# Moving the split weight rings by 32 bytes in a matmul-bound decoder layer

## The reference, cut to what matters

```
x = LN(a*x + 0.5*FFN1(x))        FFN: (silu(x @ w_gate) * (x @ w_up)) @ w_down, width 5632
x = LN(a*x + Mixer(x))
x = LN(a*x + 0.5*FFN2(x))
Mixer: z = x @ w_in -> q, k, v | c_b, c_c, c_h | g_attn, g_conv
       y_attn = differential attention (8 heads; prompt causal, sample over paged caches) @ w_attn_out
       y_conv = (c_b * short_conv(c_c * c_h)) @ w_conv_out
       (sigmoid(g_attn) * y_attn + sigmoid(g_conv) * y_conv) @ w_o
```

## Time and profile before

| | |
|---|---|
| median of 3 runs | 2275.51 us (2274.4 to 2275.91) |
| the profiled execution's own time | 2274.37 us |
| its span, first to last instruction | 2272.6 us |
| TensorE matmul busy | 2258.4 us, 18574 matmuls |
| VectorE busy | 1366.7 us |
| ScalarE busy | 998.0 us |
| DMA | 475 MB, mean 209 GB/s |

### The profile page before, as it was taken

One profiled execution on the slowest core, in us unless ns is written; L12 is line 12 of the kernel. 1 busy time (PEld: TensorE's weight loads), 2 busy tenths in 40 slices (PEclk: granted clock), 3 DMA queues, 4 the chain that ended last, 5 costly groups with the idle time before them and its releaser, 6 DMA issues.

```text
span 2272.6 us, 45670 instructions
## 1 busy us (share of the span) xinstructions
PE 2258.4 (99%) x18574; PEld 2227.3 (98%) x18574; DVE 1366.7 (60%) x1523; ACT 998.0 (44%) x1236; POOL 29.8 (1%) x59
## 2 busy tenths in 40 slices
PE   9999999999999999999999999999999999999997
PEld 9999999999999999999998899999999999999997
DVE  5444454444655689999975457886444444445554
ACT  5344444443434454455543454554444444434333
POOL 1000000000000001000000000000000000000001
PEclk9999999999999999999999999999999999999999
DMA  7655555555555688989988855555555555555553
GB/s 247 193 176 184 178 180 180 174 186 183 178 184 179 193 279 289 320 286 328 334 300 317 292 175 190 182 176 185 183 173 187 172 189 178 182 180 181 181 182 116
DMA packets 233439, 475.47 MB, mean 209 GB/s; under 512 B 18448, under 2 KB 21888, under 8 KB 233312
## 3 DMA queue, kind: packets, MB, share of 16 engines
q1 hardware_dynamic: 225920, 465.22, 61.8%
q0 software_dynamic: 2320, 5.68, 0.8%
q10 hardware_dynamic: 5072, 2.78, 0.4%
HBM read 468.13 MB, written 4.43 MB: 208 GB/s over the span
## 4 chain that ended last, share of the span: by engine, by line
PE 99%; POOL 0%; DVE 0%; issue 0%; ACT 0%; DVEq 0%; POOLq 0%
PE ps L651 31%; PE ps L650 31%; PE ps L652 31%; PE ps L764 1%; PE ps L765 1%; PE ps L766 1%; PE ps L907 1%; POOL y L633 0%; PE ps L853 0%; PE ps L795 0%; PE ps L871 0%; PE ps L870 0%; PE ps L877 0%; PE ps L886 0%; PE ps L885 0%; PE ps L884 0%
## 5 line engine op out<-in xcount | busy, mean ns | idle before, releaser
L1382 DVE TENSOR_TENSOR w_lo<-w_raw,w_hi 128x1024 fp32r<-128x1024 f32 x750 | 912.9, 1223 | 799.0 <-ACT w_hi L1004 796.3
L1004 ACT ACTIVATE w_hi<-w_raw 128x1024 fp32r<-128x1024 f32 x750 | 790.4, 1060 | 1022.6 <-PE ps L652 987.6
L652 PE MATMUL ps<-x_hi,w_lo 128*128 128x264 f32 x3840 | 1094.1, 285 | 0.0
L651 PE MATMUL ps<-x_lo,w_hi 128*128 128x264 f32 x3840 | 1092.1, 284 | 0.0
L650 PE MATMUL ps<-x_hi,w_hi 128*128 128x264 f32 x3840 | 1091.5, 284 | 0.2 <-issue 0.2
L650 PEld LDWEIGHTS ps<-x_hi,w_hi 128*128 128x128 f32 x3840 | 726.5, 189 | 12.4 <-issue 8.2
L652 PEld LDWEIGHTS ps<-x_hi,w_lo 128*128 128x128 f32 x3840 | 726.1, 189 | 0.0
L651 PEld LDWEIGHTS ps<-x_lo,w_hi 128*128 128x128 f32 x3840 | 723.5, 188 | 0.0
L651 PE MATMUL ps<-h_lo,w_hi 128*128 128x264 f32 x1408 | 400.8, 285 | 0.0
L652 PE MATMUL ps<-h_hi,w_lo 128*128 128x264 f32 x1408 | 400.4, 284 | 0.0
L650 PE MATMUL ps<-h_hi,w_hi 128*128 128x264 f32 x1408 | 398.7, 283 | 0.0
(11 more groups left out here) (268 smaller groups left out, 1372.3 us busy)
## 6 DMA issues: line engine op xcount, KB each, us to landing
w_raw<-in_ffn_w_down SPq DMA_DIRECT2D x176, 512.0 KB, 3.7
w_raw<-in_ffn_w_gate SPq DMA_DIRECT2D x175, 512.0 KB, 3.5
w_raw<-in_ffn_w_up SPq DMA_DIRECT2D x175, 512.0 KB, 4.3
w_raw<-in_w_in SPq DMA_DIRECT2D x160, 512.0 KB, 5.1
kv_ring<-in_cache_k SPq DMA_DIRECT2D x64, 512.0 KB, 6.0
kv_ring<-in_cache_v SPq DMA_DIRECT2D x64, 512.0 KB, 6.2
w_raw<-in_w_o SPq DMA_DIRECT2D x32, 512.0 KB, 4.2
w_raw<-in_w_conv_out SPq DMA_DIRECT2D x16, 512.0 KB, 5.3
```

What stands on the lines that cost most here:

```text
L651: nc.tensor.matmul(acc, wh, lo[:, kt], start=False, stop=False)
L652: return nc.tensor.matmul(acc, wl, hi[:, kt], start=False, stop=last)
L1004: nc.scalar.activation(w_hi[:, s], w_raw[:, s], ACT.Copy).then_inc(w_hi_ready, 1)
L1382: V.tensor_tensor(w_lo[:, s], w_raw[:, s], w_hi[:, s].bitcast(F32), ALU.subtract).then_inc(w_lo_ready, 1)
```

## The change

Where the two split rings begin is worked out by another rule: 208 modulo 256 takes the place of 240. Of w_hi the first byte moves from 66800 to 66768, of w_lo from 83440 to 83408. `lam` no longer stands ahead of the rings but behind them (66752 becomes 100032). `ident` and all that follows stay at the same bytes. No instruction, wait or transfer is added or removed.

```
         lam_in = at("lam_in", [HD, 4])
         lam_prod = at("lam_prod", [HD, 2])
-        lam = at("lam", [P, 4])
         SPLIT_RING = RING * KC * (WC + W_GAP)
-        w_at = -(-(top + 32) // LINE) * LINE - 32
+        w_at = -(-(top - 64) // LINE) * LINE + 64

         def spaced(flat):

...
         w_hi = spaced(at("w_hi", [P, W_FIRST + SPLIT_RING], F32R, w_at))
         w_lo = spaced(at("w_lo", [P, W_FIRST + SPLIT_RING], F32R, w_at + SPLIT_RING * 4))
         top = w_at + (W_FIRST + 2 * SPLIT_RING - W_GAP) * 4
+        lam = at("lam", [P, 4])
         ident = at("ident", [P, P])
```

## The result

The changed kernel takes 2287.74 us (2287.48 to 2288.0, 4 runs) against 2275.23 us for the kernel before beside it: ratio 1.0056, 95% interval 1.0041 to 1.0071. It is slower by 12.5 us. 2264 was forecast, a gain of 11 us; the measured time lies near rival B's 2286.

A forecast was written before the change was run, and what follows sets the result against it. TensorE bounds the kernel: number of matmuls times their start-to-start interval, plus some 14 us at the ends. 2274.37 less 11.3 = 2263.1, forecast as 2264 because that execution is 1.1 us under the median; range 2254 to 2288.

The forecast's parts named there:

- rival B: Split products at 176: weight read meets moving stream in 11 of 12 loads; 2286 us (2280 to 2298); chance 0.30.
- parts 1, 2 and 3: Nothing added or removed, only addresses differ; moving lam zero; split writes 0, ends -1 and +3 us.
- part 3: ScalarE's writes of w_hi and VectorE's of w_lo at residue 208: taken 0, ends -1 and +3 us.
- table of distances: Half chunk times by distance: 1.44 us at 80, 1.454 at 144 and 16; 1.44, 1.47, 1.44 at 208.
- Part 4: 704 chunks of rows at a fixed distance: 1.4455 us per half, gain 0.008 each, 1408 x 0.008 = 11.3 us.
- the one odd load: Last weight load of a half chunk, for the next k, at distance less 32; at 144 it costs 0.014 us.
- Part 5: Last chunk of a panel, changing k every third matmul; 78 of them, nothing taken, end 3.9 us.
- Part 6: The 16 chunks of first gate and up panels at 176, 112, 48, 240: 0, ends -0.5 and +2.5 us.
- part 7: Raw chunks, 768 matmuls at all multiples of 8, shifted by 32: 0, ends -2 and +2 us.
- Rival A: Split products: distance buys nothing, the stream at 176 settles at the same 1.454; 2275 us (2271 to 2280); chance 0.20.
- port rule: Weight loads and moving columns use separate SBUF read ports, so the change is worth 0 us; chance 0.05.
- Its sign in the profile: TensorE timeline: steps of 0.12 us gone from the middle of a half chunk would show the slower case.

The follow-up runs named there:

- the run with the weights still: Changed kernel with the weights of k = 0 in both halves of a chunk, products with k = 1 weights left out, moving tile as it should be: 2263.93 us.
- the tile still: Changed kernel with the even moving tile in both halves of a chunk, products with odd tiles left out, weights as they should be: 2266.54 us.

## Why the prediction was wrong

- **What bounds the kernel** held: TensorE alone, 2.1 us of waits, granted clock 1.00. So did parts 1, 2 and 3: the splits take what they took, VectorE is busy 95.6 of 100 us in the tight stretch, lam shows nowhere. Had the tiles' run with the rings in their old place not given the same 2288, part 3 could have been blamed.
- **The table of distances** read from the side by side stretch was right in its good and bad values (80 is at 1.441 in steady panels, too, and the run with it came within 2 us). It was right as well that the change goes where no row is. For 208, the mean over three halves, 1.450, was too high: its steady value is 1.441.
- **Part 4 is the step that failed.** I took 1.4455 us for a half, from two arguments. One was to interpolate, from 208 and 80: the table has no such smoothness, 176 is the worst of all nine values, between 144 and 208. The other was that only the one odd load of a half pays, by its own distance, and that at 144 it would be free. The odd load's distance doesn't forecast the cost: with odd loads at 144 and at 80, which the prediction had as free, steady halves at 176 and 112 take 0.027 and 0.024 more than the best, and in the run with the weights still a load at 144 at each change of chunk goes with no loss. (Whether at 144 itself the 0.014 is the price of the load at 112 or of the step that comes with it, no run parts; with the tile still that load comes once a chunk, not twice, and only 0.007 a half is lost.) Loads at 176 cost nothing in the sum where nothing steps, one ring at a time doesn't pay its share, and one step alone isn't a share of both. The cost belongs to the whole sequence. The term came out at +0.0135 us a half at 176 instead of -0.008 (1.454 less 1.4455 is in fact 0.0085, 12.0 us and not 11.3, which changes nothing here). The 626 chunks that aren't a panel's last would lose 626 x 0.027 = 17 us by it and lost 11.7: the down panels at 48 lose 0.010 a chunk, the first chunk of a feed-forward panel 0.003, and in the middle stage a steady chunk loses 0.011 in the mean, those right behind attention matmuls nothing.
- **Part 5**: the last chunks lost 0.019 us each in the gate and up panels and gained 0.03 in the down panels at 48, 1.0 us in all, taken as 0. **Part 6**: side by side +0.3 us, **part 7**: raw +0.1 us. All three are inside their ends; with part 4 they make up the 13.1 us of the span.
- **Rival A**: no. The halves didn't settle at 1.454, and addresses do have a part: kernels with the same matmuls took 2257 to 2293 us by where the weights lie against the moving tile. (Its reading in the prediction, 1.453 us for a half at 144, is 1.455 in the earlier trace rows; 1.454 in the earlier trace rows.) The port rule of the Trainium skill (TensorE: Matmul & The Clock Gate, "Step-by-step: what each phase is for") would give 2275 in every one of these kernels. The traces don't agree with it, by 18 us either way.
- **Rival B** had the time (2286) and not the mechanism, so the hit is luck: its 11 us were half of the widest price that the single 1.47 half allowed. "In 11 of 12 loads" the read at 176 was to cost by itself; the second halves without a step say no. Its sign in the profile, the even steps gone from the middle of a half, did appear, and would have confirmed the wrong reason. It deserved more than 0.30: no row held a half at 176, and the worst half on the table, the 1.47 at 208, was one with an odd load at 176.

What stays open is the mechanism behind it. No view here shows TensorE's reads of SBUF, so why a step costs next to nothing at 80 and 208, is over in four matmuls at 144 and takes twelve at 176 isn't explained here, nor is it shown that the two reads contend; a gap other than 32 bytes between weight rows wasn't tried.

## What to carry to other kernels

When TensorE is the bound, compare its start-to-start interval between stretches of the same instruction: a spread of 1% at full clock and without waits can be a matter of addresses, worth a sweep of the weights' place against the moving tiles, modulo 256 bytes here. Don't interpolate such a sweep or add it up from single loads; a few halves out of another stretch of the kernel can forecast it (80 did, 1.441) and can miss (at 208 three halves gave 1.450 for a steady 1.441, at 112 1.472 for 1.465). Measure whole panels at the new place. Hold the moving tiles and shift the rings, then hold the rings and shift the tiles: if both give the same time, it is the difference that counts, provided that no third tensor moved along.

## What the runs showed of the hardware that wasn't expected

- The time of a stream of fp32r matmuls (128 x 264, one 128 x 128 load each) depends on the difference of the addresses of the moving tile and of the weights: 0.1201 us a matmul at best, 0.1223 at worst with both rings at one distance, 1.8%, with no wait and the clock at 1.00.
- The stream has a memory over a dozen matmuls, and can hold two different rates at the same addresses: 3658 and 3585 matmuls in 440 us of the same loop, 2% apart. What went before them is the difference that is known. In a complete kernel too: down panels at 240 take 1.459 and 1.454 us a half.
- Eight columns less (256 for 264) saved 1.2 ns of a matmul at distance 80; at 264 the steps were an even 0.120 us, at 256 they weren't even.
